# Triangular inversion in a recurrent layer: the second and third product of a level become one product of a buffer with itself

## The chip, the cores and the metric

The kernel runs on one core of a Trainium2 chip. The metric is the device time of one execution in microseconds (us); lower is better. The engines of the core are TensorE (PE; its weight loads are shown apart as PEld), VectorE (DVE), ScalarE (ACT), GpSimd (POOL) and the queues that issue transfers (SP's above all).

## The reference, cut to what matters

The whole program is three transformer blocks over 256 tokens of width 1024. The change lies in the first one, in the RWKV-7 recurrence of 8 heads with 64 columns each:

```
def step(state, inp):
    rt, wt, kt, vt, at, bt = inp
    sa = jnp.einsum('bhvk,bhk->bhv', state, at)
    state = state * wt[:, :, None, :] + sa[..., None] * bt[:, :, None, :] + vt[..., None] * kt[:, :, None, :]
    return state, jnp.einsum('bhvk,bhk->bhv', state, rt)
```

The kernel does not walk through the 256 tokens. It takes chunks of 128 tokens, builds for each of the 2 chunks x 8 heads a strictly triangular 128 x 128 matrix of the products between tokens, and needs the inverse of identity minus that matrix. These are 16 inverses.

## The kernel before

One program is written out for each engine; the engines meet at semaphores. The order on an engine is the order in which its functions are called, nothing is scheduled afterwards. The stage in question comes after the projections of the first block (`pe_mats` builds the 16 matrices) and before the recurrences (`pe_recurrences`), which use the inverses.

**The inversion** (`pe_inverse`, `act_inverse`, `dve_inverse`, `pool_inverse`) doubles the size of the inverted diagonal blocks in seven levels, 1, 2, 4 up to 64 on a side. The 16 matrices are handled as `NG` = 4 groups of four; a group is one instruction of 128 x 512 on DVE, ACT or POOL, and on TensorE four fp32 matmuls of 128 x 128, of which each shows as two passes in the profile (8 rows of LDWEIGHTS and MATMUL). `TI` holds the inverse so far, `TJ` its transpose, `AAB` the matrices. Per level from 1 on, for each group:

- POOL masks `AAB` with the block pattern of the level into `ALA` (L1087). It may write once the first product of the level before has been read.
- First product (L1098): `ALA` times `TI` into PSUM. It waits for the mask and for `TI` of the level before.
- ACT copies all of it to `PP` (L1125), once `TJ` of the level before is there too.
- Second product (L1109): `PP` with `TJ`. Third product (L1116): `TJ` with `PP`, its transpose. Level 6 has no third product, since `TI` isn't needed behind it.
- DVE adds the third to `TI` (L1157) and the second to `TJ` (L1159), each 128 x 512, from PSUM and SBUF.

On TensorE all four groups' first products stand ahead of the second and third ones of the level. At the head of levels 2 and 3 DVE also works off `dve_bonus` (L1133, L1137, L1139, L1141), four operations of 128 x 512 between SBUF buffers that prepare the layer's output and have nothing to do with the inversion; they stand in its queue before the additions of that level. The eight PSUM banks are taken in turn. `SM` is a small buffer of 64 columns of constants. `sp_start` issues the early loads on SP's queue, the constants (L722) among them, behind the vectors (L701 to L720) and ahead of the small weights of the layer.

Of the kernel before, what the change touches and what calls it, by code (L numbers as in the profile page):

```python
# [7 lines left out]
P = 128  # L8
# [5 lines left out]
ALU = mybir.AluOpType  # L14
# [12 lines left out]


NAMES = (["ident", "cinc", "cexc", "strict", "incl", "heads"]
         + [f"lvl{i}" for i in range(7)] + [f"acc{i}" for i in range(7)] + ["after", "upto", "ones", "swap"])  # L30
COLS = {n: 128 * i for i, n in enumerate(NAMES)}
WIDE = 128 * len(NAMES)

# [1 line left out]
def constants():  # L35
    s = np.arange(128)[:, None]
    t = np.arange(128)[None, :]
    out = {"ident": s == t, "strict": s < t, "incl": s <= t, "heads": s // 64 == t // 64,
           "cinc": (s <= t) * 1.0 - (s < 64), "cexc": (s < t) * 1.0 - (s < 64),
           "after": s > t, "upto": s <= t, "ones": (s >= 0) & (t >= 0), "swap": s == (t + 64) % 128}  # L40
    for i in range(7):
        m = 1 << i
        same = s // (2 * m) == t // (2 * m)
        right = (t // m) % 2 == 1

        out[f"lvl{i}"] = same & right & ((s // m) % 2 == 0)
        edge = t // (2 * m) * (2 * m) + m

        out[f"acc{i}"] = np.where(right, (s >= edge) & (s <= t), (s > t) & (s < edge))
    return np.concatenate([out[n].astype(np.float32) for n in NAMES], 1)  # L50
# [143 lines left out]
def program(nc, a):  # L194
    ctx = ExitStack()
    with ctx:
# [14 lines left out]
        XL = sb("XL", [P, 8, S], F32R)  # L211
        XT = (XH, XL)
        TF = sb("TF", [P, 2, 512])
        CST = sb("CST", [P, WIDE])
        VEC = sb("VEC", [P, 2, P])
        GB = sb("GB", [P, 2, D])
        SM = sb("SM", [P, 64])
# [453 lines left out]
        def group(x, g):  # L671
            return x[:, 4 * g:4 * g + 4, :]
# [20 lines left out]
        def sp_start(e):  # L693
# [13 lines left out]
            for r, name, n in ((0, "rwkv_mu", 1792), (15, "rwkv_k_k", 512), (19, "rwkv_k_a", 512),  # L707
# [11 lines left out]
                        ).then_inc(*up("rows", by=16))  # L719
            e.dma_start(VR[112:120, 1, :], a["c_2"].rearrange("a (r p) -> (a r) p", p=P)  # L720
                        ).then_inc(*up("rows", "rows", by=16))
            e.dma_start(CST[:, P:], a["consts"][:, P:]).then_inc(*up("consts", "consts", by=16))  # L722
            e.dma_start(GW2[0:16, :], a["gla_gate_w2"][0]).then_inc(*up("even", by=16))
            e.dma_start(W2A2[0:64, :], a["rwkv_w2"][0]).then_inc(*up("even", by=16))
            e.dma_start(W2A2[64:128, :], a["rwkv_a2"][0]).then_inc(*up("even", by=16))
# [346 lines left out]
                k.then_inc(*up("masked", use, ("free", use)))  # L1072


        def pool_inverse(e):
            for lv in range(7):
                for g in range(NG):
                    if lv == 0:
                        e.wait_ge(*at(("m", 4 * g + 3)))
                        if g == 0:  # L1080
                            e.wait_ge(*at(("bt", 3)))
                            e.wait_ge(*at(("la", 1)))
                    else:
                        e.wait_ge(*at(("p done", lv - 1, g)))
                        if lv == 1:
                            e.wait_ge(*at(("tj", 0, g)))
                    e.tensor_tensor(group(ALA, g), group(AAB, g), bc(f"lvl{lv}"), ALU.mult).then_inc(  # L1087
                        *up("level", ("al", lv, g)))

        def pe_inverse(e):  # L1090
            for lv in range(7):
# [9 lines left out]
                if lv == 0:  # L1101
                    continue
                for g in range(NG):
                    b = bank(e, ("j", lv, g))
                    e.wait_ge(*at(("pp", lv, g)))
                    if g == NG - 1:
                        e.wait_ge(*at(("tj", lv - 1, g)))
                    for s in range(4):
                        k = e.matmul(b[:, s * P:s * P + P], group(PP, g)[:, s, :], TJ[:, 4 * g + s, :],  # L1109
                                     start=True, stop=True)  # L1110
                    if lv == 6:
                        k.then_inc(*up("inverse", ("full", ("j", lv, g))))
                        continue
                    b = bank(e, ("i", lv, g))
                    for s in range(4):
                        k = e.matmul(b[:, s * P:s * P + P], TJ[:, 4 * g + s, :], group(PP, g)[:, s, :],  # L1116
                                     start=True, stop=True)
                    k.then_inc(*up("inverse", ("full", ("i", lv, g)), ("full", ("j", lv, g))))

        def act_inverse(e):  # L1120
            for lv in range(1, 7):
                for g in range(NG):
                    e.wait_ge(*at(("full", ("p", lv, g))))
                    e.wait_ge(*at(("tj", lv - 1, g)))
                    e.activation(group(PP, g), four(("p", lv, g)), ACT.Copy).then_inc(  # L1125
                        *up("levels", ("pp", lv, g), ("free", ("p", lv, g))))

        def dve_bonus(e, t):
# [14 lines left out]
        def dve_inverse(e):  # L1143
# [7 lines left out]
            for lv in range(1, 7):  # L1151
                if lv in (2, 3):
                    dve_bonus(e, lv - 2)
                for g in range(NG):
                    e.wait_ge(*at(("full", ("j", lv, g))))
                    if lv < 6:
                        e.tensor_tensor(flat(group(TI, g)), ps(("i", lv, g)), flat(group(TI, g)), ALU.add).then_inc(  # L1157
                            *up("tij", ("ti", lv, g), ("free", ("i", lv, g))))
                    e.tensor_tensor(flat(group(TJ, g)), ps(("j", lv, g)), flat(group(TJ, g)), ALU.add).then_inc(  # L1159
                        *up("tij", ("tj", lv, g), ("free", ("j", lv, g))))  # L1160


        def pe_chunk(e, step):
# [1350 lines left out]
```

## Time and profile before

| | us |
|---|---|
| time before, median of 3 runs (1250.09 to 1251.1) | 1250.32 |
| the profiled execution, its own time | 1247.66 |
| its span | 1245.7 |
| from the first second product to the end of the inversion on TensorE | 163.9 to 221.2 |
| TensorE busy over the whole span | 1128.2 (91%) |
| DVE, ACT, POOL busy | 742.0, 519.2, 120.8 |

The profile shows one execution. Shares of busy time are averages over the whole program; what bounds one stage is read from the rows of that stage: from the chain of work that ended last, the timelines of the engines, and the table by stretches. A granted clock of 1.00 means TensorE at 2.4 GHz, 0.50 means 1.2 GHz.

### The profile page before, as it was taken

What the parts mean: (1) busy time and instruction counts of PE and PEld (TensorE: products, weight loads), DVE (VectorE), ACT (ScalarE), POOL (GpSimd) and SP (SyncE); (2) the same over time, 40 slices, a digit from 0 to 9 for tenths busy, and PEclk for the clock granted to TensorE, in tenths of its full rate; (3) what the DMA queues carried; (4) which work ended last, traced back from release to release, by engine and by line L of the source; (5) the groups of instructions that cost most, each with busy time, mean ns of one, the idle gap of its engine ahead of it and who ended that gap; (6) DMA issues with size and microseconds to landing.
All of it is one profiled execution on the core that took longest, in us unless ns stands there. A gap on an engine that the chain in (4) does not pass through costs nothing.

```text
span 1245.7 us, 17256 instructions
## 1 busy us (share of the span) xinstructions
PE 1128.2 (91%) x7196; PEld 997.8 (80%) x7196; DVE 742.0 (60%) x1046; ACT 519.2 (42%) x710; POOL 120.8 (10%) x115
## 2 busy tenths in 40 slices
PE   5989799996799999977979499999969996999997
PEld 5788699995699998756767399998749875999885
DVE  3486585437676666566664666666574565666433
ACT  3452422124444443334564344343355565555331
POOL 0005163210300000040000300000010000000000
PEclk8899999958799999987999799999979997999999
DMA  8345000004398677531693287768615322565550
GB/s 279 101 123 184 16 2 1 1 1 163 107 300 273 210 262 273 203 120 53 182 195 123 83 285 243 242 235 299 230 40 182 105 88 68 171 195 177 203 169 34
DMA packets 112270, 193.68 MB, mean 155 GB/s; under 512 B 4514, under 2 KB 84913, under 8 KB 112066
## 3 DMA queue, kind: packets, MB, share of 16 engines
q1 hardware_dynamic: 108530, 179.65, 43.2%
q0 software_dynamic: 3248, 11.83, 4.3%
q8 instruction: 57, 0.93, 0.3%
q10 hardware_dynamic: 416, 1.11, 0.2%
q14 instruction: 19, 0.16, 0.0%
HBM read 188.38 MB, written 4.19 MB: 155 GB/s over the span
## 4 chain that ended last, share of the span: by engine, by line
PE 82%; DVE 10%; ACT 5%; issue 2%; SPq 1%; DMA 0%; POOL 0%; ACTq 0%; DVEq 0%
PE ps L406 22%; PE ps L407 21%; PE ps L408 21%; PE ps L1098 2%; PE ps L1868 2%; PE ps L1109 2%; PE ps L1853 2%; PE ps L1116 1%; DVE XL L539 1%; PE ps L1335 1%; DVE ARR L390 1%; DVE AR L1071 1%; PE ps L1846 1%; DVE STAT L556 1%; PE ps L1290 1%
## 5 line engine op out<-in xcount | busy, mean ns | idle before, releaser
L390 DVE TENSOR_TENSOR ARR<-ring,ARR 128x2048 fp32r<-128x2048 f32 (+1 forms) x147 | 329.3, 2246 | 220.9 <-ACT ARR L379 220.8
L406 PE MATMUL ps<-XH,ARR 128*128 128x256 f32 x1232 | 354.9, 288 | 25.6 <-DVE ARR L390 13.4
L379 ACT ACTIVATE ARR<-ring 128x2048 fp32r<-128x2048 f32 (+1 forms) x147 | 274.8, 1875 | 214.8 <-PE ps L408 163.5
L407 PE MATMUL ps<-XL,ARR 128*128 128x256 f32 x1232 | 351.9, 286 | 0.0
L408 PE MATMUL ps<-XH,ARR 128*128 128x256 f32 x1232 | 351.4, 285 | 0.0
L406 PEld LDWEIGHTS ps<-XH,ARR 128*128 128x128 f32 x1232 | 238.2, 193 | 30.9 <-issue 27.9
L407 PEld LDWEIGHTS ps<-XL,ARR 128*128 128x128 f32 x1232 | 238.4, 194 | 0.1
L408 PEld LDWEIGHTS ps<-XH,ARR 128*128 128x128 f32 x1232 | 238.2, 193 | 0.0
L406 PE MATMUL ps<-ARR 128*128 128x512 f32 x420 | 170.4, 406 | 9.1 <-DVE ARR L491 5.8
L407 PE MATMUL ps<-ARR 128*128 128x512 f32 x420 | 167.2, 398 | 0.0
L408 PE MATMUL ps<-ARR 128*128 128x512 f32 x420 | 167.1, 398 | 0.0
L406 PEld LDWEIGHTS ps<-ARR 128*128 128x128 f32 x420 | 80.0, 191 | 34.7 <-issue 9.5
L408 PEld LDWEIGHTS ps<-ARR 128*128 128x128 f32 x420 | 79.9, 190 | 19.0
L407 PEld LDWEIGHTS ps<-ARR 128*128 128x128 f32 x420 | 80.0, 190 | 18.2 <-issue 0.5
L406 PE MATMUL ps<-ARR,XH 128*128 128x512 f32 (+1 forms) x128 | 50.8, 397 | 7.0 <-DVE XL L539 5.4
L1513 DVE SCALAR_TENSOR_TENSOR AR<-ring,AR 128x1024 f32<-128x1024 f32 x42 | 53.9, 1283 | 1.1
L407 PE MATMUL ps<-ARR,XH 128*128 128x512 f32 (+1 forms) x128 | 49.9, 390 | 0.0
L408 PE MATMUL ps<-ARR,XL 128*128 128x512 f32 (+1 forms) x128 | 49.6, 388 | 0.0
L1603 ACT ACTIVATE ARR<-XN 128x512 fp32r<-128x512 f32 x22 | 13.9, 632 | 79.9 <-DVE XN L1621 79.9
L469 PE MATMUL ps<-CST,XN 128*128 128x128 f32 x96 | 18.6, 353 | 31.3 <-ACT XN L2071 19.4
L469 PEld LDWEIGHTS ps<-CST,XN 128*128 128x128 f32 x96 | 14.6, 182 | 35.5 <-ACT XN L2071 20.7
L1087 POOL TENSOR_TENSOR AR<-AR,CST 128x512 f32<-128x512 f32 x28 | 37.6, 1365 | 47.1 <-DVE AR L1071 25.3
(335 smaller groups left out, 1337.3 us busy)
## 6 DMA issues: line engine op xcount, KB each, us to landing
ring<-in_ffn_w_gate_up_dram SPq DMA_DIRECT2D x44, 1024.0 KB, 5.7
ring<-in_w_dram SPq DMA_DIRECT2D x32, 1024.0 KB, 5.2
ring<-in_w_ada_dram SPq DMA_DIRECT2D x24, 1024.0 KB, 5.3
ring<-in_ffn_w_down_dram SPq DMA_DIRECT2D x22, 1024.0 KB, 5.1
ring<-in_even_w_in_dram SPq DMA_DIRECT2D x13, 1024.0 KB, 5.6
ring<-in_w_in_dram SPq DMA_DIRECT2D x9, 1024.0 KB, 5.4
ring<-in_mla_w_q_b_dram SPq DMA_DIRECT2D x6, 768.0 KB, 4.7
ring<-in_even_w_out_dram SPq DMA_DIRECT2D x4, 1024.0 KB, 4.9
```

The costliest lines, as they stand in the source:

```text
L379: e.activation(split(i)[0], raw(i), ACT.Copy).then_inc(*up("hi", ("hi", i)))
L390: e.tensor_tensor(lo, raw(i), hi.bitcast(F32), ALU.subtract).then_inc(*up("lo", ("lo", i), ("raw free", i)))
L406: e.matmul(out, lhs[0], rhs[0], start=first, stop=False)
L407: e.matmul(out, lhs[0], rhs[1], start=False, stop=False)
L408: return e.matmul(out, lhs[1], rhs[0], start=False, stop=last)
L469: k = e.transpose(ps((tag, c // 2))[:, o:o + P], src[:, t, c * P:(c + 1) * P], ident)
L1087: e.tensor_tensor(group(ALA, g), group(AAB, g), bc(f"lvl{lv}"), ALU.mult).then_inc(*up("level", ("al", lv, g)))
L1098: k = e.matmul(b[:, s * P:s * P + P], ALA[:, 4 * g + s, :], ident if lv == 0 else TI[:, 4 * g + s, :], start=True, stop=True)
L1109: k = e.matmul(b[:, s * P:s * P + P], group(PP, g)[:, s, :], TJ[:, 4 * g + s, :], start=True, stop=True)
L1513: k = e.scalar_tensor_tensor(acc, w[:, c, :], CSL[:, k0 + c:k0 + c + 1], acc, ALU.mult, ALU.add)
L1853: k = e.matmul(b[:, TILE[t]], A.q_of(i, t), A.k_of(i, P * (t + 1)), start=True, stop=True)
L1868: k = e.matmul(ps((A.tag, "o", g))[64 * (h % 2):64 * (h % 2) + 64, o + P * t:o + P * t + P], A.v_of(h, j), px[:, (t + j) * P:(t + j) * P + ...
```

## The change

From level 1 on, `PP` becomes a buffer of two interleaved sides. At level `lv` the columns of a matrix are cut in blocks of `1 << lv`; the even blocks are side 0, the odd ones side 1. ACT writes side 1 of `PP` from side 1 of `TJ` (SBUF to SBUF) and side 0 from side 0 of the first product (PSUM to SBUF). TensorE multiplies this buffer with itself: one product per group in place of two. Its columns of side 1 carry what the second product gave and those of side 0 what the third gave, each in the rows of the other side; the remaining rows hold products that are not wanted. DVE adds the two halves with a mask by rows: a scalar_tensor_tensor that multiplies by a column of zeros and ones from `SM` and adds, 128 x 256 each. The masks are 14 new columns of the constants, which come with a transfer of their own on SP's queue.

```diff
+            e.dma_start(CST[:, P:], a["consts"][:, P:WIDE - P]).then_inc(*up("consts", by=16))
+            e.dma_start(SM[:, 8:22], a["consts"][:, COLS["sides"]:COLS["sides"] + 14]).then_inc(
+                *up("consts", "consts", by=16))
...
+        def side(x, lv, which):
+            return x.rearrange("p s (b w t) -> p s b w t", w=2, t=1 << lv)[:, :, :, which, :]
+
+        def rows_on(lv, which):
+            return SM[:, 8 + 2 * lv + which:9 + 2 * lv + which]
...
                 for g in range(NG):
-                    b = bank(e, ("j", lv, g))
+                    b = bank(e, ("ji", lv, g))
                     e.wait_ge(*at(("pp", lv, g)))
-                    if g == NG - 1:
-                        e.wait_ge(*at(("tj", lv - 1, g)))
                     for s in range(4):
-                        k = e.matmul(b[:, s * P:s * P + P], group(PP, g)[:, s, :], TJ[:, 4 * g + s, :],
-                                     start=True, stop=True)
-                    if lv == 6:
-                        k.then_inc(*up("inverse", ("full", ("j", lv, g))))
-                        continue
-                    b = bank(e, ("i", lv, g))
-                    for s in range(4):
-                        k = e.matmul(b[:, s * P:s * P + P], TJ[:, 4 * g + s, :], group(PP, g)[:, s, :],
-                                     start=True, stop=True)
-                    k.then_inc(*up("inverse", ("full", ("i", lv, g)), ("full", ("j", lv, g))))
+                        w = PP[:, 4 * g + s, :]
+                        k = e.matmul(b[:, s * P:s * P + P], w, w, start=True, stop=True)
+                    k.then_inc(*up("inverse", ("full", ("ji", lv, g))))
...
         def act_inverse(e):
             for lv in range(1, 7):
                 for g in range(NG):
+                    e.wait_ge(*at(("tj", lv - 1, g)))
+                    e.activation(side(group(PP, g), lv, 1), side(group(TJ, g), lv, 1), ACT.Copy).then_inc(*up("levels"))
+                for g in range(NG):
                     e.wait_ge(*at(("full", ("p", lv, g))))
-                    e.wait_ge(*at(("tj", lv - 1, g)))
-                    e.activation(group(PP, g), four(("p", lv, g)), ACT.Copy).then_inc(
+                    e.activation(side(group(PP, g), lv, 0), side(four(("p", lv, g)), lv, 0), ACT.Copy).then_inc(
                         *up("levels", ("pp", lv, g), ("free", ("p", lv, g))))
...
                 for g in range(NG):
-                    e.wait_ge(*at(("full", ("j", lv, g))))
+                    use = ("ji", lv, g)
+                    e.wait_ge(*at(("full", use)))
                     if lv < 6:
-                        e.tensor_tensor(flat(group(TI, g)), ps(("i", lv, g)), flat(group(TI, g)), ALU.add).then_inc(
-                            *up("tij", ("ti", lv, g), ("free", ("i", lv, g))))
-                    e.tensor_tensor(flat(group(TJ, g)), ps(("j", lv, g)), flat(group(TJ, g)), ALU.add).then_inc(
-                        *up("tij", ("tj", lv, g), ("free", ("j", lv, g))))
+                        x = side(group(TI, g), lv, 0)
+                        e.scalar_tensor_tensor(x, side(four(use), lv, 0), rows_on(lv, 1), x, ALU.mult, ALU.add).then_inc(
+                            *up("tij", ("ti", lv, g)))
+                    x = side(group(TJ, g), lv, 1)
+                    e.scalar_tensor_tensor(x, side(four(use), lv, 1), rows_on(lv, 0), x, ALU.mult, ALU.add).then_inc(
+                        *up("tij", ("tj", lv, g), ("free", use)))
```

TensorE at level 1 before, from the last two first products on (L1098), with the second (L1109) and third products (L1116) of the groups in turn:

```order
672 L1098 MATMUL ps<-AR 128x128 [waits s_tij,s_level,s_masked]
673 L1098 MATMUL ps<-AR 128x128 x3
674 L1109 MATMUL ps<-AR 128x128 [waits s_levels,s_tij]
675 L1109 MATMUL ps<-AR 128x128 x3
676 L1116 MATMUL ps<-AR 128x128 [waits s_tij]
677 L1116 MATMUL ps<-AR 128x128 x3
678 L1109 MATMUL ps<-AR 128x128 [waits s_levels,s_tij]
679 L1109 MATMUL ps<-AR 128x128 x3
```

TensorE at the same place now; L1110 is the first product and L1120 the product of `PP` with itself:

```order
672 L1110 MATMUL ps<-AR 128x128 [waits s_tij,s_level,s_masked]
673 L1110 MATMUL ps<-AR 128x128 x3
674 L1120 MATMUL ps<-AR 128x128 [waits s_levels,s_tij]
675 L1120 MATMUL ps<-AR 128x128 x3
676 L1120 MATMUL ps<-AR 128x128 [waits s_levels,s_tij]
677 L1120 MATMUL ps<-AR 128x128 x3
678 L1120 MATMUL ps<-AR 128x128 [waits s_levels,s_tij]
679 L1120 MATMUL ps<-AR 128x128 x3
680 L1120 MATMUL ps<-AR 128x128 [waits s_levels,s_tij]
681 L1120 MATMUL ps<-AR 128x128 x3
682 L1110 MATMUL ps<-AR 128x128 [waits s_tij,s_level,s_levels]
```

The first products of the next level follow after four products instead of eight.

ACT before, over all six levels: one copy per group and level (L1125).

```order
72 L1039 ACTIVATE XN<-XN,SM 128x256 [waits s_low]
73 L1125 ACTIVATE AR<-ps 128x512 [waits s_tij,s_inverse] x24
74 L1302 ACT_TABLE_LOAD [waits s_inverse]
```

ACT now at levels 1 to 3: L1127 copies the side of `TJ`, L1130 that of the first product.

```order
73 L1127 ACTIVATE AR<-AR 128x128x2 [waits s_tij] x4
74 L1130 ACTIVATE AR<-ps 128x128x2 [waits s_inverse] x4
75 L1127 ACTIVATE AR<-AR 128x64x4 [waits s_tij] x4
76 L1130 ACTIVATE AR<-ps 128x64x4 [waits s_inverse] x4
77 L1127 ACTIVATE AR<-AR 128x32x8 [waits s_tij] x4
```

All four copies of `TJ`, which wait for DVE's last addition of the level before, now stand ahead of the copies of the first products.

## Rows read from the trace of the kernel before

**Rows 1.** The page: busy time, share of the span, instructions of each engine.

```profile
PE 1128.2 (91%) x7196; PEld 997.8 (80%) x7196; DVE 742.0 (60%) x1046; ACT 519.2 (42%) x710; POOL 120.8 (10%) x115
```

**Rows 2.** The chain that ended last, levels 1 and 2: start, us, what.

```profile
164.07 0.89 PE ps L1109 x8
164.96 0.89 PE ps L1116 x8
...
171.21 3.57 PE ps L1098 x32
...
221.24 1.79 PE ps L1290 x16
```

**Rows 3.** Timeline of TensorE: start, us, engine, line, form, count.

```profile
163.90 1.06 PE L1109 MATMUL ps<-AR 128*128 128x128 f32 x8
...
171.05 1.17 PE L1098 MATMUL ps<-AR 128*128 128x128 f32 x9
```

**Rows 4.** Groups by line and shape from 163.9 to 221.2: busy us, mean ns.

```profile
L1116 PE MATMUL ps<-AR 128*128 128x128 f32 x160 | 21.1, 275 | 0.0
...
L1125 ACT ACTIVATE AR<-ps 128x512 f32<-128x512 f32 x21 | 12.5, 597 | 43.0 <-PE ps L1098 43.0
...
L1137 DVE TENSOR_TENSOR AR<-AR 128x512 f32<-128x512 f32 x2 | 3.3, 1644 | 0.1
```

**Rows 5.** Timeline of DVE around the extra work of levels 2 and 3.

```profile
171.25 0.69 DVE L1157 TENSOR_TENSOR AR<-ps,AR 128x512 f32<-128x512 f32 x1 [0.50 <-PE ps L1116]
171.86 0.68 DVE L1159 TENSOR_TENSOR AR<-ps,AR 128x512 f32<-128x512 f32 x1
172.46 1.55 DVE L1133 TENSOR_TENSOR AR<-AR 128x512 f32<-128x512 f32 x1
...
178.98 0.68 DVE L1157 TENSOR_TENSOR AR<-ps,AR 128x512 f32<-128x512 f32 x1
...
183.16 0.67 DVE L1159 TENSOR_TENSOR AR<-ps,AR 128x512 f32<-128x512 f32 x1
183.76 0.97 DVE L1133 TENSOR_TENSOR AR<-AR 128x512 f32<-128x512 f32 x1
...
189.70 0.68 DVE L1157 TENSOR_TENSOR AR<-ps,AR 128x512 f32<-128x512 f32 x1
```

**Rows 6.** Timeline of POOL, the masks of levels 3 to 5.

```profile
172.19 6.32 POOL L1087 TENSOR_TENSOR AR<-AR,CST 128x512 f32<-128x512 f32 x4 [4.45 <-PE ps L1098]
182.91 6.32 POOL L1087 TENSOR_TENSOR AR<-AR,CST 128x512 f32<-128x512 f32 x4 [4.40 <-PE ps L1098]
193.63 4.96 POOL L1087 TENSOR_TENSOR AR<-AR,CST 128x512 f32<-128x512 f32 x4 [4.40 <-PE ps L1098]
```

**Rows 7.** Groups elsewhere with the shapes and kinds that the change adds.

```profile
L795 DVE SCALAR_TENSOR_TENSOR AR<-AR,VEC 128x256 f32<-128x256 f32 x14 | 6.8, 485 | 0.5
...
L1258 DVE TENSOR_TENSOR XN<-XN,AR 128x512 f32<-128x512 f32 x2 | 1.4, 692 | 0.1
...
L1724 DVE TENSOR_TENSOR AR<-AR 128x256 f32<-128x256 f32 x2 | 0.8, 419 | 0.0
...
L1241 ACT ACTIVATE XN<-ps 128x256 f32<-128x256 f32 x4 | 1.5, 383 | 13.3 <-PE ps L1203 8.9 <-PE ps L1200 4.4
```

**Rows 8.** Busy us by stretch: PE, PEld, DVE, ACT, POOL; granted clock, DMA, GB/s.

```profile
152.00:155.40 3.40, 1.36 (x10) 1.20 (x11) 3.40 (x11) 0.00 (x0) 1.26 (x1) 1.00 0.00 0
155.40:158.80 3.40, 3.33 (x16) 3.06 (x15) 3.40 (x5) 0.00 (x0) 2.41 (x2) 0.50 0.00 0
158.80:162.20 3.40, 2.47 (x18) 1.95 (x17) 2.63 (x3) 1.25 (x3) 2.02 (x3) 1.00 0.00 0
...
244.10:281.70 37.60, 37.60 (x168) 33.78 (x170) 13.29 (x22) 6.71 (x9) 7.50 (x6) 0.50 0.00 1
```

**Rows 9.** SP's queue, and the chain's first users of the constants (L823).

```profile
13.73 0.36 SPq L722 DMA_DIRECT2D CST<-in_consts_dram  x1
...
41.57 1.05 PE ps L823 x2
```

More of the change, by code:

```diff
@@ L29 @@
 NAMES = (["ident", "cinc", "cexc", "strict", "incl", "heads"]
-         + [f"lvl{i}" for i in range(7)] + [f"acc{i}" for i in range(7)] + ["after", "upto", "ones", "swap"])
+         + [f"lvl{i}" for i in range(7)] + [f"acc{i}" for i in range(7)] + ["after", "upto", "ones", "swap", "sides"])
 COLS = {n: 128 * i for i, n in enumerate(NAMES)}
@@ L39, in constants @@
            "cinc": (s <= t) * 1.0 - (s < 64), "cexc": (s < t) * 1.0 - (s < 64),
-           "after": s > t, "upto": s <= t, "ones": (s >= 0) & (t >= 0), "swap": s == (t + 64) % 128}
+           "after": s > t, "upto": s <= t, "ones": (s >= 0) & (t >= 0), "swap": s == (t + 64) % 128,
+           "sides": (s >> np.minimum(t // 2, 6)) % 2 == t % 2}
     for i in range(7):
@@ L213, in program @@
         TF = sb("TF", [P, 2, 512])
-        CST = sb("CST", [P, WIDE])
+        CST = sb("CST", [P, WIDE - P])
         VEC = sb("VEC", [P, 2, P])
@@ L721, in sp_start @@
                         ).then_inc(*up("rows", "rows", by=16))
-            e.dma_start(CST[:, P:], a["consts"][:, P:]).then_inc(*up("consts", "consts", by=16))
+            e.dma_start(CST[:, P:], a["consts"][:, P:WIDE - P]).then_inc(*up("consts", by=16))
+            e.dma_start(SM[:, 8:22], a["consts"][:, COLS["sides"]:COLS["sides"] + 14]).then_inc(
+                *up("consts", "consts", by=16))
             e.dma_start(GW2[0:16, :], a["gla_gate_w2"][0]).then_inc(*up("even", by=16))
```

## The prediction

> **What bounds the kernel now.** I read the page first: TensorE is busy for 91% of the span [rows 1]. Then the chain of waits at the place of the change: from 163 us to 221 us it never leaves TensorE. Per level it shows four first products of 0.89 us (3.57 us in one piece), then second and third products in turn, 0.89 us each, eight of them, and straight behind the inversion the next stage's matmuls [rows 2]. So a level takes 12 x 0.893 = 10.72 us, and a product removed here is time removed, as long as the other engines keep up with the shorter level. The groups by line and the timelines say how busy they are: DVE's additions take 0.69 us each [rows 5], POOL's masks 1.2 to 1.6 us [rows 6], ACT's copies 0.597 us, and of these 57 us ACT idles 43 waiting for first products [rows 4]. The timelines of DVE and POOL also show the one place where they are nearly full: the extra work in levels 2 and 3 [rows 5, 6].
>
> **What is removed.** The third products, levels 1 to 5, four groups each: 20 groups (160 passes in the rows [rows 4]) x 0.893 us = 17.9 us, all of it on the path. The product that stays has the size of the second one, with the buffer on both sides; nothing in the rows gives a reason for another duration. The level becomes 8 x 0.893 = 7.15 us. Level 6 had no third product and keeps its length. Now the engines that must follow in 7.15 us.
>
> **DVE, ordinary levels.** Two scalar_tensor_tensor of 128 x 256 per group replace two additions of 128 x 512. The trace doesn't show this form with PSUM and short runs. Nearest: a scalar_tensor_tensor of 128 x 256 with a column operand, 0.485 us; an addition of 128 x 256 whose output steps over every second element (rotary embedding), 0.419 us [rows 7]; the old 512-wide one, 0.69 us [rows 5], as the upper end. I take 0.485. Additions in a row start 0.61 us apart at 0.69 us each (171.25, 171.86 [rows 5]), so 0.08 overlaps and the new ones start 0.40 apart. A group costs 0.80, below the 0.893 of its product; a level 3.2 us of 7.15. `TI` of group 3 is done 0.2 + 0.49 = 0.7 us after the last product's slot (0.2 as from 171.05 [rows 3] to 171.25 [rows 5]), but TensorE wants it only after three further first products, 2.7 us. Cost nothing; cover gone, it would be 0.7 us per level.
>
> **ACT.** Eight copies of 128 x 256 at 0.383 us [rows 7] are 3.1 us of 7.15; at the 0.597 of the old copy, 4.8. They stand in a new order: all four of `TJ` first, the last of which waits for DVE's last addition. That is done 0.2 + 0.40 + 0.49 = 1.1 us into the first products; then one `TJ` copy and one copy of a first product end at 1.9 us (2.3 at the upper end), and the product with itself starts at 3.57. Nothing again, hidden behind four first products. What waits behind it is the release of the first product's PSUM bank, wanted eight products later.
>
> **POOL.** Four masks take 5.0 us undisturbed and 6.3 us beside DVE's extra work [rows 6], below 7.15. They start about 1.1 us into the level (172.19 against 171.05) and are wanted one level on. Nothing.
>
> **DVE in levels 2 and 3** is where I expect part of the gain to stay. The four extra operations run from 172.46 to 178.98, 6.5 us, and the second time from 183.76 to 189.70, 5.9 us [rows 5], against a level that is now 7.15 us and also wants 3.2 us of additions. By hand, in times of this execution: the first product with itself can start at 163.9, where the second product started; four take 3.6 us, so level 2's first products start at 167.5 instead of 171.05 [rows 3]. DVE starts level 1's last additions at 167.7, the extra work at 168.5, and ends it at 175.0. The first `TI` is done at 175.5; level 3's first product could start at 174.65. **Stall 0.9 us.** Eight additions follow; the second extra work starts at 175.0 + 3.2 = 178.2. Level 4's first product could start at 175.55 + 7.15 = 182.7. If the extra work takes 5.9 us again, `TI` is done at 184.6, a stall of 1.9. But it is POOL that makes these operations slow (1.64 us [rows 4], a like one elsewhere 0.692 [rows 7]), and POOL now starts its masks at 176.7, 1.5 us ahead of the extra work instead of 0.85 us, and is done earlier with respect to it; I take 5.5 us. **Stall 1.5 us.** Bounds: 1.0 (5.0 us) and 2.5 (6.5 us, as the first time). Behind each stall the late `TJ` lets the product with itself begin with the fourth first product's end at best: 0 to 0.2 us more. From level 4 on the spare time above applies.
>
> At this place the rows say that additions from PSUM take 0.67 to 0.69 us whether POOL runs (183.16) or not (171.25), and that SBUF-only ones don't [rows 5, 6]. The Trainium skill, page "SBUF — State Buffer", section "Summary: rules for kernel authors", gives a harder rule: when a VectorE instruction has two SBUF inputs and GpSimd reads SBUF, the second to issue waits until the first has finished. An estimate by that rule would put full masks and extra operations end to end, some 6.0 us for the second extra work, a stall of 2.0 instead of 1.5 and a time 0.5 us above mine. The first time, end to end would be 4 x 1.24 + 4 x 0.61 = 7.4 us; the trace has 6.8 (172.19 to 178.98 [rows 5, 6]), so the rule is a little too hard here.
>
> **The early transfer.** 14 columns for 128 partitions on SP's queue cost one issue, 0.36 us in the row ahead of it [rows 9], ahead of the small weights and of the fourth ring load. Those weights are first used at 41.6 us [rows 9], more than 20 us later. Bounds 0 and 0.4 us; I take 0.1. `SM` is otherwise untouched, and banks are taken in turn as before, the last eight before the recurrences being again level 6's.
>
> **Sum.** 17.9 - 0.9 - 1.5 - 0.2 (the products behind the stalls, the transfer) = 15.3 us. Behind the inversion the chain stays on TensorE [rows 2], which is busy for all of the 37.6 us from 244.1 on [rows 8], and the next stage's loads are released by the same queues, so the gain should pass to the end undiminished. The profiled execution would go from 1247.66 to 1232.4; the runs' median, 2.7 us above it, from 1250.32 to **1235.0 us**. With my bounds (stalls 1.9 to 3.4 us, 0 to 0.4 behind them, transfer 0 to 0.4) 1234.3 to 1236.6; with the 512-wide duration for the additions, see the second rival, 1238.5.
>
> **Rivals.**
>
> 1. *The clock behind the inversion falls or returns at other work.* It falls at 244.1 and comes back at 281.7 us, 37.6 us at half speed with TensorE on the chain [rows 8]. The work arrives 15 us earlier, so the change of clock may meet other matmuls. Each us of full-clock work moved into or out of that stretch is worth 1 us. Against a large effect: what precedes the fall (small matmuls behind a wait for DVE) stays the same work, and the three runs lie within 1.0 us. For: the stretch is long, and there is denser work within it. An earlier return by 3 to 10 us of work gives 1225 to 1232 (chance 0.07); a later one or an earlier fall, 2 to 5 us, gives 1237 to 1240 (0.08).
>
> 2. *DVE becomes the pace.* If the new operation costs 0.69 us, starts lie 0.60 apart: 1.2 us per group against 0.893. The first `TI` comes 0.2 later, the second extra work starts 1.6 later, and the fourth `TI` holds the fourth first product by about 0.9 in both levels: together near 3.6 us, 1238.5. If it also had to take turns with POOL, as the SBUF-only operations do at 1.64 instead of 0.69 [rows 4, 7], four masks would add up to 4 x 0.95 = 3.8 us to DVE's 3.2 in an ordinary level, 7.0 of 7.15, and some 2 us to each of levels 2 and 3: 1239. Against: its first input is PSUM, as in the additions that POOL doesn't slow. Chance 0.07.
>
> 3. *Slower than before: the stalls cost the clock.* After a stretch in which TensorE worked only 1.36 of 3.4 us the clock fell for 3.4 us; after one with 2.47 of 3.4 the products ran on at full speed [rows 2, 8]. My stalls (0.9 and 1.5 us in long dense work) resemble the second. If the fall came at level 4 and stayed, as it does from 244 on, the 24 products left (21.4 us) would take 21.4 us more: 1235.0 + 21.4 = 1256. The point from which the change loses is 15.3 us of full-clock work done at half. Against: dense products brought the clock back at once at 158.8. Chance 0.03; a single short fall, worth 1.7 us, lies in my range.
>
> 4. *It doesn't do what it says:* a wait elsewhere takes the gain, the inversion being shorter but the recurrences starting when they did. Nothing in the chain behind 221.2 comes from another engine's earlier work [rows 2]. 1248 to 1252, chance 0.02.
>
> **How the numbers follow.** The forecast, 1233 to 1237, has 0.73; the rivals 0.15, 0.07, 0.03, 0.02. The range 1230 to 1239 takes in the first, most of the second and the near half of the clock cases, and leaves out some 0.15. Time can be told from no change here beyond 0.2%, 2.5 us. Faster: 0.73 + 0.15 + 0.07 = 0.95; within 0.2%: 0.02; slower: 0.03.
>
> **What would show it.** The chain between 160 and 206 us all TensorE but for two short pieces with DVE, before the first products of levels 3 and 4; the product with itself at 0.89 us per group, 192 passes; scalar_tensor_tensor near 0.485 us at every level, the one with runs of two elements included; the inversion ending near 206 us; the stretch at half clock again about 37 us. Wrong would be: an addition above 0.6 us, a stall of TensorE in levels 5 or 6, or a span behind the inversion that is not the old one.

## The result and the profile after

| | before | changed |
|---|---|---|
| median of 4 runs, us | 1250.2 (1250.08 to 1251.1) | 1232.74 (1232.04 to 1233.0) |
| the profiled execution, its own time | 1247.66 | 1232.66 |
| its span | 1245.7 | 1230.8 |

The ratio is 0.9858 with a 95% interval of 0.9841 to 0.9875: 17.5 us faster, where 15.3 were forecast. The profiled executions differ by 15.0 us. That these two numbers are not the same turned out to be the interesting part.

The timeline of TensorE after the change (start, us, engine, line, form, count), from the last passes of level 1's first products to the next stage (L1298), answers to [rows 3]; L1110 is the first product, L1120 the product of `PP` with itself:

```profile
162.87 3.74 PE L1120 MATMUL ps<-AR 128*128 128x128 f32 x32
166.44 3.74 PE L1110 MATMUL ps<-AR 128*128 128x128 f32 x32
170.02 3.74 PE L1120 MATMUL ps<-AR 128*128 128x128 f32 x32
173.69 3.81 PE L1110 MATMUL ps<-AR 128*128 128x128 f32 x32
177.34 3.74 PE L1120 MATMUL ps<-AR 128*128 128x128 f32 x32
182.58 3.81 PE L1110 MATMUL ps<-AR 128*128 128x128 f32 x32 [1.51 <-DVE AR L1164]
186.23 3.74 PE L1120 MATMUL ps<-AR 128*128 128x128 f32 x32
...
204.10 1.95 PE L1298 MATMUL ps<-CST,AR 128*128 128x128 f32 x16
```

Starts of the blocks lie 3.57 us apart: a level takes 7.15 us, as worked out. Two places are longer. Level 3's first products start at 173.69 where 170.02 + 3.57 = 173.59 was possible, and level 4's at 182.58 instead of 177.34 + 3.57 = 180.91: stalls of 0.10 and 1.67 us, with 0.08 us behind each where the product with itself follows (177.34 - 173.69 = 3.65). The inversion from its first such product to the next stage takes 204.1 - 162.9 = 41.2 us. Before it was 221.1 - 163.9 = 57.2 us [rows 2, 3]. The stage gave 16.0 us.

DVE's timeline (same columns) shows the two pieces of extra work (L1138 to L1146) between the masked additions (L1164, L1167), to be read against [rows 5]:

```profile
167.05 0.47 DVE L1167 SCALAR_TENSOR_TENSOR AR<-ps,SM,AR 128x256 f32<-128x256 f32 x1
167.44 0.68 DVE L1138 TENSOR_TENSOR AR<-AR 128x512 f32<-128x512 f32 x1
168.15 1.64 DVE L1142 TENSOR_TENSOR AR<-AR 128x512 f32<-128x512 f32 x1
...
173.07 0.47 DVE L1164 SCALAR_TENSOR_TENSOR AR<-ps,SM,AR 128x256 f32<-128x256 f32 x1
...
176.21 1.75 DVE L1138 TENSOR_TENSOR AR<-AR 128x512 f32<-128x512 f32 x1
...
181.35 0.69 DVE L1146 TENSOR_TENSOR AR<-AR 128x512 f32<-128x512 f32 x1
181.96 0.48 DVE L1164 SCALAR_TENSOR_TENSOR AR<-ps,SM,AR 128x256 f32<-128x256 f32 x1
```

POOL's masks at the same places, the counterpart of [rows 6]:

```profile
167.58 6.69 POOL L1099 TENSOR_TENSOR AR<-AR,CST 128x512 f32<-128x512 f32 x4 [0.86 <-PE ps L1110]
174.90 5.86 POOL L1099 TENSOR_TENSOR AR<-AR,CST 128x512 f32<-128x512 f32 x4 [0.63 <-PE ps L1110]
```

The first extra work takes 173.07 - 167.44 = 5.6 us instead of the 6.5 of before, since its first operation now starts 0.14 us ahead of POOL's mask and runs in 0.68 us; before, POOL started 0.27 us ahead (172.19, 172.46 [rows 5, 6]) and it took 1.55. The second takes 181.96 - 176.21 = 5.75 us. Which of its four operations is the fast one can change from run to run: here the last took 0.69 us and the first 1.75, in the third trace of this kernel the first took 0.68 and the last 1.64, though POOL had started 1.31 us ahead in both.

Groups by line and shape inside the inversion (count, then busy us, mean ns, idle us before them and its releaser), the counterpart of [rows 4]:

```profile
L1120 PE MATMUL ps<-AR 128*128 128x128 f32 x192 | 22.4, 275 | 0.0
...
L1110 PE MATMUL ps<-AR 128*128 128x128 f32 x162 | 19.2, 276 | 1.5 <-DVE AR L1164 1.5
...
L1167 DVE SCALAR_TENSOR_TENSOR AR<-ps,SM,AR 128x256 f32<-128x256 f32 x23 | 10.9, 475 | 4.4 <-PE ps L1120 4.4
L1164 DVE SCALAR_TENSOR_TENSOR AR<-ps,SM,AR 128x256 f32<-128x256 f32 x20 | 9.6, 479 | 9.5 <-PE ps L1120 9.3
L1127 ACT ACTIVATE AR<-AR 128x256 f32<-128x256 f32 x20 | 8.3, 417 | 19.0 <-DVE AR L1167 19.0
L1130 ACT ACTIVATE AR<-ps 128x256 f32<-128x256 f32 x21 | 7.5, 379 | 5.0 <-PE ps L1110 5.0
```

The passes that are left kept their 275 ns, the additions take 0.48 us, the copies 0.38 and 0.42 us.

The rest of the span moved too. It is best read in three parts, each bounded by a start on TensorE:

| profiled execution, us | before | changed | difference |
|---|---|---|---|
| up to the first second product / product with itself | 163.9 | 162.9 | -1.0 |
| the inversion from there | 57.2 | 41.2 | -16.0 |
| from the next stage's start to the end | 1024.6 | 1026.7 | +2.1 |

Nothing in the first and third part was changed but one small transfer. Their granted clock differs. By stretches (start and end, length, then PE, PEld, DVE, ACT, POOL busy; granted clock, DMA share, GB/s), first early in the program, before:

```profile
15.00:22.30 7.30, 6.04 (x29) 6.04 (x30) 2.69 (x6) 0.00 (x0) 0.00 (x0) 0.53 0.94 308
```

The same stretch after:

```profile
15.00:22.30 7.30, 6.22 (x35) 6.23 (x36) 2.51 (x6) 0.00 (x0) 0.00 (x0) 1.00 0.98 293
```

And behind the inversion, before (its long half-clock stretch is in [rows 8]) and then after:

```profile
281.70:298.70 17.00, 8.60 (x65) 7.41 (x63) 15.97 (x24) 9.33 (x24) 1.18 (x2) 0.80 0.45 154
```

```profile
204.10:225.60 21.50, 20.70 (x181) 19.57 (x179) 11.98 (x18) 3.75 (x7) 8.94 (x5) 1.00 0.00 1
225.60:263.10 37.50, 37.50 (x155) 33.19 (x155) 11.63 (x19) 6.69 (x9) 4.80 (x3) 0.50 0.00 0
263.10:283.60 20.50, 11.95 (x86) 10.77 (x84) 18.24 (x27) 9.46 (x25) 3.87 (x5) 0.75 0.36 131
```

Early on, the execution of before ran 29 passes, nearly all at half clock, where the changed one ran 35 at full clock. That this makes the 1.0 us of the first part is not shown: over the 14 traces of this document that part takes 162.8 to 164.2 us without following its time at half clock (23.9 to 30.7 us; the shortest start has 30.7).

Behind the inversion the half-clock stretch is as long (37.5 against 37.6 us) and begins 21.5 instead of 23.0 us behind its end; a further piece at half clock follows. Summed from the trace's clock record to the end, the third part holds 148.5 us at half clock in place of 144.8. In the run with all extra work in one level (below) 3.4 us at half clock cost dense matmuls 1.7 us; an estimate at that rate gives 1.8 of the 2.1 us.

### The profile page after: what moved, and what is told of

Read it like the earlier page. It is cut to its first block, busy times and chain, and to the rows that moved or that the text cites. A ratio compares the mean times of both kernels' runs of the same rounds, so it can differ in the third digit from the quotient of the medians.

```text
span 1230.8 us, 16937 instructions
## 1 busy us (share of the span) xinstructions
PE 1110.9 (90%) x7036; PEld 981.1 (80%) x7036; DVE 732.1 (59%) x1046; ACT 522.8 (42%) x734; POOL 120.7 (10%) x115
## 4 chain that ended last, share of the span: by engine, by line
PE 80%; DVE 11%; ACT 5%; issue 2%; SPq 1%; DMA 0%; POOL 0%; ACTq 0%; DVEq 0%
PE ps L407 22%; PE ps L408 21%; PE ps L409 21%; PE ps L1876 2%; PE ps L1861 2%; PE ps L1110 1%; DVE XL L540 1%; PE ps L1343 1%; DVE ARR L391 1%; DVE AR L1074 1%; PE ps L1854 1%; PE ps L1120 1%; DVE STAT L557 1%; PE ps L1298 1%; ACT ARR L380 1%
## 5 line engine op out<-in xcount | busy, mean ns | idle before, releaser
L409 PEld LDWEIGHTS ps<-ARR 128*128 128x128 f32 x420 | 80.0, 190 | 18.8
L470 PE MATMUL ps<-CST,XN 128*128 128x128 f32 x96 | 18.3, 354 | 30.1 <-ACT XN L2079 12.6
L600 POOL TENSOR_TENSOR X<-XN,GB 128x1024 f32<-128x1024 f32 x6 | 14.1, 2343 | 279.4 <-ACT XN L578 279.4
```

The costliest lines, as they stand in the source:

```text
L409: return e.matmul(out, lhs[1], rhs[0], start=False, stop=last)
L470: k = e.transpose(ps((tag, c // 2))[:, o:o + P], src[:, t, c * P:(c + 1) * P], ident)
L600: e.tensor_tensor(X[:, t, :], XN[:, t, :], GB[:, 0, :], ALU.mult).then_inc(*up("affine"))
```

## The experiments

Two theories. **A**: the gain is the stage's, 17.9 us of products less the stalls behind DVE's extra work, and everything else only scatters. **C**: on top of it the change puts the end of the inversion at another offset to the changes of TensorE's clock, and with that the rest of the program gets systematically shorter or longer. In the expectations a rival B stands for the first form of C. "Stage" is the inversion as above and "rest" what follows it, both from the profiled execution; means are over all runs of a kernel.

### The changed kernel again

The same file, twice more, each time beside other runs of before.

> The changed kernel as it is, to see what of its gain belongs to the change and what to the clock's position in one execution. Theory A (17.9 us of products removed, 1.9 us given back in two stalls behind DVE's extra work, nothing elsewhere on average): 15.9 to 16 us faster than before, ratio 0.9872. Rival B (the gain is larger than the inversion's own, since behind it or ahead of it less is spent at half clock): the ratio stays at 0.986 or below, and the stretches at half clock are shorter in sum than before.

> The changed kernel once more, since its runs of the second job lay in two groups, spans of 1220 to 1225 and of 1233 us, while the stage takes 41.2 us in both traces. Theory A (stage alone): 16 us below before on average, 1232 to 1234. Theory C (on top of the stage, the work behind the inversion now more often meets the clock at a better offset, rest of the program 1019 us long instead of 1024 to 1028): mean 18 to 21 us below before, again in two groups.

Ratios 0.9833 (0.9798 to 0.9869) and 0.9851 (0.9822 to 0.988): the second mean lies 18.8 us below the runs of before beside it, as theory C had it and more than A's 16. The stage was 41.2 and 41.1 us, the rest 1027.6 and 1026.2 us in the profiled executions. Rival B's second sign, less time at half clock, is missing in these traces; both come from the slower group of runs. The runs lay at 1222.4 to 1226.7 (four) and 1234.7, 1234.9; then 1224.7, 1224.8 and 1232.1 to 1234.2 (four). The kernel before was not as steady either as its first runs had it: 63 more runs gave 1241.8 to 1252.5. Over all runs: changed 1230.0 (16 runs), before 1248.8 (67 runs), 18.7 us apart, of which the stage explains 16.0. The six runs of the changed kernel at 1222.4 to 1226.7 had a mean granted clock of 0.932 to 0.938, the other ten 0.927 to 0.934; none of the six was profiled.

### Only the products back

```diff
                         k = e.matmul(b[:, s * P:s * P + P], w, w, start=True, stop=True)
+                    if lv < 6:
+                        for s in range(4):
+                            w = PP[:, 4 * g + s, :]
+                            k = e.matmul(b[:, s * P:s * P + P], w, w, start=True, stop=True)
```

> The changed kernel with the product of the buffer with itself computed twice in levels 1 to 5, so TensorE has as much to do as before while ACT, DVE and the early transfer are those of the change. Theory A: 20 products of 0.893 us come back and cover the stalls: the time of before, 1250 us, within 1 us; the inversion 57.3 us. Rival (part of the gain comes from the smaller copies and additions, or from the clock): 2 us or more below the time of before.

Ratio 1.0009 (0.9992 to 1.0026), stage 57.2 us, exactly that of before. Its timeline of TensorE has the two products in turn and no stall, as in [rows 3]:

```profile
163.10 1.06 PE L1120 MATMUL ps<-AR 128*128 128x128 f32 x8
163.99 1.06 PE L1124 MATMUL ps<-AR 128*128 128x128 f32 x8
...
170.25 3.74 PE L1110 MATMUL ps<-AR 128*128 128x128 f32 x32
173.82 1.06 PE L1120 MATMUL ps<-AR 128*128 128x128 f32 x8
```

All of the stage's gain is in the 20 products; the smaller copies and additions bring nothing by themselves.

### Only the narrower additions

```diff
-                        e.tensor_tensor(flat(group(TI, g)), ps(("i", lv, g)), flat(group(TI, g)), ALU.add)
+                        x = side(group(TI, g), lv, 0)
+                        e.tensor_tensor(x, side(four(("i", lv, g)), lv, 0), x, ALU.add)
...
-                    e.tensor_tensor(flat(group(TJ, g)), ps(("j", lv, g)), flat(group(TJ, g)), ALU.add)
+                    x = side(group(TJ, g), lv, 1)
+                    e.tensor_tensor(x, side(four(("j", lv, g)), lv, 1), x, ALU.add)
```

> The kernel before with only its additions narrowed to the side that a level changes (128 x 256 instead of 128 x 512); three products, copies and transfers as before. Theory A: DVE is not on the chain of the stage, no change: within 1 us of 1250. Rival (the additions' width matters): 1 to 3 us faster.

Ratio 0.9997 (0.998 to 1.0015), stage 57.2 us. Its additions by group (columns as above):

```profile
L1164 DVE TENSOR_TENSOR AR<-ps,AR 128x256 f32<-128x256 f32 x23 | 9.6, 416 | 4.6 <-PE ps L1112 4.6
L1161 DVE TENSOR_TENSOR AR<-ps,AR 128x256 f32<-128x256 f32 x20 | 8.5, 424 | 27.2 <-PE ps L1119 27.1
```

DVE worked 0.42 us instead of 0.69 per addition and idled the difference (27.2 us before one of the two groups, 16.5 in the trace of before). It was not on the chain.

### Only the transfer

```diff
+            e.dma_start(SM[:, 8:22], a["consts"][:, COLS["sides"]:COLS["sides"] + 14]).then_inc(
+                *up("consts", "consts", by=16))
```

> The kernel before with only the new transfer of 14 mask columns on the SP queue and the shorter constants buffer. Forecast: 0 to 0.4 us slower, not to be told from no change. Rival: the transfer delays what follows on the queue or shifts the start, 1 us or more either way; the trace then shows the first second product at another time than 163.9 us.

Ratio 0.9994 (0.998 to 1.0009); the first second product starts at 163.3 us. The start in all the traces, with the transfer or without, lies between 162.8 and 164.2. So it costs nothing that can be seen, and a shift of 1 us either way, as the rival had it, is scatter that kernels without the transfer show too.

### DVE's extra work: spread, before and after the change

```diff
-                if lv in (2, 3):
-                    dve_bonus(e, lv - 2)
+                if lv in (2, 3, 4, 5):
+                    dve_bonus(e, (lv - 2) // 2, (0, 1) if lv % 2 == 0 else (2, 3))
```

where the last argument picks two of the four operations.

> The changed kernel with DVE's extra work (eight operations, four each at the head of levels 2 and 3) spread as two each over levels 2 to 5. Theory A: DVE then needs 3.3 + 3.2 us of a level's 7.15, both stalls (0.1 and 1.7 us) go, the inversion takes 39.5 us from the first product with itself to the next stage instead of 41.4, time 1.8 us below the changed kernel. Rival: the stall is not the extra work's but the new order on ACT (all copies of TJ ahead): then a stall of 1 to 2 us stays in levels 3 or 4 and the time is that of the changed kernel.

> The changed kernel with DVE's extra work as two operations each at the head of levels 2 to 5, again beside the changed kernel on one chip. Theory A: 1.9 us below the changed kernel in the mean, the stage 39.3 us again. Theory C: the stage is 1.9 us shorter for certain, but the mean of the whole lies within 3 us of the changed kernel either way, since the end of the inversion meets the clock at another offset.

> The kernel before with the extra work spread over levels 2 to 5. Theory A: it hid behind 10.7 us levels and costs nothing there, so the time stays 1250.2 within 1 us. Rival: it cost time before too, 1 us or more faster.

In the changed kernel both stalls go: every block of TensorE now lies 3.57 us behind the last, and the stage is 39.3 us in both traces, 1.9 less, as theory A had it:

```profile
170.49 3.74 PE L1120 MATMUL ps<-AR 128*128 128x128 f32 x32
174.06 3.74 PE L1110 MATMUL ps<-AR 128*128 128x128 f32 x32
177.63 3.74 PE L1120 MATMUL ps<-AR 128*128 128x128 f32 x32
181.21 3.74 PE L1110 MATMUL ps<-AR 128*128 128x128 f32 x32
```

That rules out the new order on ACT as the cause of the stall; it is unchanged here. The time of the whole is less clear. Ratios to before 0.9851 (0.9827 to 0.9875) and 0.9835 (0.9806 to 0.9865), mean 1228.8 over 12 runs against 1230.0 of the changed kernel: in the right direction, within the scatter. In the kernel before the same edit leaves the stage at 57.2 us and the time at 0.9997 (0.9982 to 1.0012): the extra work cost nothing while a level was 10.7 us long.

### All extra work in one level

```diff
-                if lv in (2, 3):
-                    dve_bonus(e, lv - 2)
+                if lv == 3:
+                    dve_bonus(e, 0)
+                    dve_bonus(e, 1)
```

> The changed kernel with all eight extra operations of DVE in front of level 3's additions instead of four each at levels 2 and 3. Theory A: DVE's 11 to 12 us of extra work start 1 us into level 3 and hold level 4's first product by some 5 to 6 us, in place of 0.1 and 1.7: 3.5 to 4.5 us above the changed kernel, if the clock stays. Rival (the prediction's third: a wait of this length makes the clock fall): a stretch at 0.50 behind the wait and 1.7 us or more on top, 1238 or above.

Mean 1236.0, 6.0 above the changed kernel, ratio 0.9902 (0.9878 to 0.9926); the trace is of the fastest of the six runs. The stage is 45.0 us, 3.7 above the changed kernel. The timeline of TensorE splits it:

```profile
178.15 3.74 PE L1120 MATMUL ps<-AR 128*128 128x128 f32 x32
185.69 5.44 PE L1110 MATMUL ps<-AR 128*128 128x128 f32 x32 [3.80 <-DVE AR L1165]
190.96 3.74 PE L1120 MATMUL ps<-AR 128*128 128x128 f32 x32
```

The first product starts at 185.69 instead of 181.72: 4.0 us of wait, not 5 to 6, since the last three extra operations ran at 0.69 us once POOL was done. Then the block needs 5.27 us to the next one's start instead of 3.57. So the 3.7 us are within what theory A expected, but made of 2.0 us of wait and 1.7 of something else. The table by stretches says of what (columns as above):

```profile
182.70:186.10 3.40, 0.41 (x4) 0.44 (x5) 3.30 (x7) 0.13 (x1) 0.00 (x0) 1.00 0.00 0
186.10:189.50 3.40, 3.40 (x19) 3.40 (x18) 2.18 (x6) 2.19 (x6) 1.65 (x2) 0.51 0.00 0
189.50:193.00 3.50, 3.50 (x33) 3.50 (x33) 0.93 (x3) 0.80 (x3) 3.33 (x3) 0.99 0.00 0
```

After 3.4 us in which TensorE worked 0.41, the clock was at half for 3.4 us, and back. A wait of 4 us cost 1.7 more in clock, while the changed kernel's stall of 1.67 cost none; where between the two the cost begins is not shown. This is the first link of the prediction's third rival; the second, that the clock stays down, did not happen between dense products. The whole stayed below the 1238 that the rival had for this case.

### Wider masked additions

```diff
-                        x = side(group(TI, g), lv, 0)
-                        e.scalar_tensor_tensor(x, side(four(use), lv, 0), rows_on(lv, 1), x, ALU.mult, ALU.add)
+                        x = flat(group(TI, g))
+                        e.scalar_tensor_tensor(x, ps(use), rows_on(lv, 1), x, ALU.mult, ALU.add)
```

and the same for `TJ`.

> The changed kernel with both masked additions over all 512 columns instead of the side's 256: this also adds the products' unwanted columns, so the inverses are not those of the reference; it prices the width. Theory A with the prediction's second rival: 0.69 us each and 0.61 apart, 1.2 us per group against 0.893: the second extra work starts 1.6 us later, and the fourth addition holds the fourth first product in levels 3 and 4; together 3.6 us above the changed kernel, 1236.3. Rival (covered by the first products as before): within 1 us of the changed kernel.

This kernel adds the unwanted columns of the products too, so its inverses are not the right ones and it serves as a price only. The stage is 46.0 us, 4.8 above the changed kernel; I had 3.6. An addition takes 0.74 us, not 0.69, and they start 0.66 apart, so in levels 3 and 4 the first products come at DVE's pace, one group per 1.32 us:

```profile
175.78 1.13 PE L1110 MATMUL ps<-AR 128*128 128x128 f32 x8 [1.53 <-DVE AR L1164]
177.10 1.13 PE L1110 MATMUL ps<-AR 128*128 128x128 f32 x8 [0.19 <-DVE AR L1164]
178.42 1.13 PE L1110 MATMUL ps<-AR 128*128 128x128 f32 x8 [0.19 <-DVE AR L1164]
```

So the halving of the additions, worth nothing alone, is worth 4.8 us once the product is gone. Yet the whole is 1230.0 in the median and 1232.7 in the mean, only 2.7 above the changed kernel. The stage and the whole part ways again, which leads to the last pair.

### The end of the inversion moved on purpose

Both kernels get matmuls computed twice at level 6, results unchanged; they only push the inversion's end. Before, five of them:

```diff
-                    for s in range(4):
+                    for s in [0, 1, 2, 3] + [0, 1, 2, 3, 0] * (lv == 6 and g == 0):
                         k = e.matmul(b[:, s * P:s * P + P], group(PP, g)[:, s, :], TJ[:, 4 * g + s, :],
```

> The kernel before with five matmuls of level 6 computed twice (1.12 us more of TensorE at the end of the inversion, result unchanged). It makes the inversion as long as to put its end at the same offset to the clock's changes as the changed kernel has. Theory A: 1.1 us slower than before, 1249.5 to 1250. Theory C: part of the runs has the short rest of 1019 us, so the mean falls below before by 1 to 4 us although work was added; a group of runs at 1240 to 1242.

The changed kernel, ten of them:

```diff
-                    for s in range(4):
+                    for s in [0, 1, 2, 3] + [0, 1, 2, 3] * (lv == 6 and g < 2) + [0, 1] * (lv == 6 and g == 2):
                         w = PP[:, 4 * g + s, :]
                         k = e.matmul(b[:, s * P:s * P + P], w, w, start=True, stop=True)
```

> The changed kernel with ten matmuls of level 6 computed twice (2.23 us more at the end of the inversion, result unchanged), which puts the inversion's end back at the offset to the clock's changes that it had before the change. Theory A: 2.2 us above the changed kernel in each of its groups, two groups as before. Theory C: the fast group thins out or goes, mean 4 to 7 us above the changed kernel, 13 to 14 us below before, runs between 1230 and 1237.

**The kernel before with 1.1 us more work is faster**: median 1242.9 against 1250.0, ratio 0.9966 (0.9944 to 0.9988), nine of its 12 runs between 1241.2 and 1243.5. Its stage is 58.3 us, as it must be; the rest is 1019.3 us instead of 1024.6. By stretches from the inversion's end on:

```profile
221.50:243.10 21.60, 20.80 (x181) 19.67 (x180) 12.14 (x18) 3.75 (x7) 8.94 (x5) 1.00 0.00 1
243.10:253.30 10.20, 10.20 (x40) 8.68 (x42) 1.54 (x3) 0.60 (x1) 0.86 (x1) 0.50 0.01 2
253.30:263.60 10.30, 10.30 (x82) 9.26 (x80) 7.44 (x13) 2.45 (x4) 2.71 (x2) 1.00 0.00 0
263.60:273.80 10.20, 10.20 (x52) 9.27 (x53) 3.85 (x6) 3.55 (x4) 2.90 (x3) 0.50 0.01 2
```

The clock falls 21.6 us behind the end as it did in the changed kernel's trace, but comes back after 10.2 us, where [rows 8] has 37.6 us at half clock without a break. Over the 90 us behind the inversion, first of the kernel before, then with the five:

```profile
221.10:311.10 90.00, 79.46 (x467) 70.93 (x466) 48.09 (x68) 23.47 (x44) 17.69 (x12) 0.75 0.17 55
```

```profile
221.50:311.50 90.00, 79.42 (x494) 69.83 (x493) 50.46 (x69) 24.50 (x44) 17.59 (x12) 0.83 0.19 64
```

The changed kernel with 2.2 us more went the other way: mean 1235.4, no run below 1232.8, which is 5.4 us for 2.2 us of work, ratio 0.9893 (0.9872 to 0.9913), rest 1028.3 us. Theory A had 1249.5 to 1250 for the first kernel and the lower group of runs still there in the second. The first result contradicts it clear of noise. The second is weaker by itself: six runs, and ten of the changed kernel's 16 lay above 1232 as well.

That it is the clock which makes the rest longer or shorter can be read from all 14 traces. The rest ranges from 1018.7 to 1028.3 us and its time at half clock from 131.6 to 152.1 us. The rest less half of that time is 951.5 to 953.0 us in 13 of them and 954.5 in the other, whatever the kernel.

All kernels together. "At half clock" is how much of the rest the clock record has at half clock, "mean - stage" what the rest and the beginning take on average:

| kernel | runs | stage | rest in its trace | at half clock | mean | mean - stage |
|---|---|---|---|---|---|---|
| before | 67 | 57.2 | 1024.6 | 144.8 | 1248.8 | 1191.6 |
| products back | 12 | 57.2 | 1024.5 | 145.0 | 1249.2 | 1192.0 |
| narrower additions | 12 | 57.2 | 1026.5 | 148.2 | 1248.4 | 1191.2 |
| transfer alone | 12 | 57.2 | 1024.4 | 144.8 | 1248.0 | 1190.8 |
| before, spread | 10 | 57.2 | 1025.9 | 147.7 | 1248.0 | 1190.8 |
| before, five more | 12 | 58.3 | 1019.3 | 134.1 | 1244.7 | 1186.4 |
| changed | 16 | 41.2 | 1026.7, 1027.6, 1026.2 | 148.5, 152.1, 148.8 | 1230.0 | 1188.8 |
| changed, ten more | 6 | 43.4 | 1028.3 | 152.1 | 1235.4 | 1192.0 |
| changed, spread | 12 | 39.3 | 1018.9, 1025.4 | 131.7, 141.8 | 1228.8 | 1189.5 |
| changed, wide additions | 6 | 46.0 | 1018.7 | 131.6 | 1232.7 | 1186.7 |
| changed, one level | 6 | 45.0 | 1019.9 | 134.6 | 1236.0 | 1191.0 |

The five kernels with a stage of 57.2 us agree within 1.2 us in the last column, whatever they do in it. Those with another length range over 5.6 us. The change's 18.7 us are thus 16.0 of the stage and some 2.7 from outside it. The 2.7 are the difference of means over runs that spread by 12.6 us, so they are uncertain by about 2, and that they are the clock's is argued from the runs' granted clock, since no trace has the lower group.

That more or less work in front changes how much of the rest runs at half clock is shown by the kernel with five more matmuls. How is not settled; theory C's offset of the inversion's end to the clock's changes does not order the traces by itself. The first fall behind the inversion comes 21.5 to 24.8 us behind its end. In two traces it came at almost the same distance (21.5 and 21.6 us) and the clock stayed down for 37.5 us in one and 10.2 in the other; the four short rests have it at 21.6, 21.7, 23.6 and 23.6 us, and long ones have it at 21.5 and 23.4.

The version with the extra work spread has the shortest stage of all and is the one to keep; against the changed kernel its advantage is shown for the stage (1.9 us) and not for the whole.

## Why the prediction was right, point by point

The measured 1232.74 lies 2.3 us below the forecast and within its range. The stage was foreseen within 0.7 us by the right mechanism. That the whole lay in the range was in part luck: the mean of all 16 runs is 1230.0, its lower edge, and six of them lay below it; the first four all came from the slower group. The second set's median alone, 1225.9, would have been outside.

- **What is removed**: 17.9 us. Held to the last digit: 192 passes left, a level at 7.15 us.
- **DVE in ordinary levels, ACT, POOL**: 0.48 us per masked addition at every level, runs of two elements included (forecast 0.485); no wait of TensorE for ACT. The wider experiment shows that the cover was real and thin.
- **First stall**: forecast 0.9, measured 0.10. The failing term is the 6.5 us of the extra work, taken from a row in which POOL's mask started first. Shorter additions let DVE start it 1.0 us into the level instead of 1.4, ahead of POOL's 1.14, so one of four operations ran in 0.68 us: 5.6 us. The prediction asked this question for the second piece only, although its own times (DVE at 168.5, POOL 1.1 us behind 167.5) had the two change places.
- **Second stall**: forecast 1.5, measured 1.67, from 5.75 us of extra work (forecast 5.5). The Trainium skill's rule ("SBUF — State Buffer", "Summary: rules for kernel authors": the second to issue waits for the first to finish) gave an estimate of 6.0; the measurement lies midway. For the first piece, where DVE's operation issued first and took 0.68 us, the trace agrees with the rule that only the second one waits; my row had POOL first.
- **Behind the stalls and the transfer**: 0.2 forecast, 0.16 and nothing visible.
- **Sum of the stage**: 15.3 forecast, 16.0 measured.
- **"The gain should pass to the end undiminished"**: the weakest step. In the profiled pair 1.0 us came on top ahead of the stage and 2.1 were lost behind it; over all runs 2.7 came on top. The prediction had named a span behind the inversion that is not the old one as a sign of being wrong, and it came: 1026.7 against 1024.6. Rival 1 named the mechanism, and its 0.15 was too little: six of 16 runs lay where its earlier return (0.07) would put them, or lower, and the scatter stands beside the forecast, not in place of it. The argument against it that failed was "the three runs lie within 1.0 us": further runs of the same kernel spread over 10.7 us.
- **From the profiled execution to the median**: I added the 2.7 us by which the profiled execution of before lay below its median. The changed one's lay 0.1 below. That alone moves the result 2.6 us below the forecast, the stage 0.7 us more, and the profiled pair's remainder (-1.0 and +2.1) takes 1.1 back: together the 2.3 us between 1235.0 and 1232.74, within 0.1.
- **Rival 2** would have cost 4.8, not 3.6 us; **rival 3** was seen behind a wait of 4 us and not behind one of 1.67, and lost 1.7 us there and not 21; **rival 4** did not occur.

## What to carry to other kernels

When a product leaves a chain, the engines that idled beside it become the next question; work out for each what it must do in the shorter period, and look for one-off work in its queue. For two engines that slow each other, a duration from the trace may not hold once their order changes: the same operation took 1.55 us behind POOL's start and 0.68 ahead of it. Judge a change of 1 to 2% by the length of its stage in two traces as well as by the whole, since what follows moved here by up to 9.6 us on the clock alone.

## What the runs showed of the hardware that I had not expected

- The same work behind the inversion took between 1018.7 and 1028.3 us, by how much of it (131.6 to 152.1 us) ran at half clock. Delaying it by 1.1 us of matmuls made the whole shorter, by 7 us in the median and 4 in the mean of the runs.
- The clock's changes are not tied to the start of the program: the kernel before had a half-clock stretch from 15.4 to 22.3 us, the changed one none until 44.7, with the same work there. The Trainium skill says so ("TensorE: Matmul & The Clock Gate", "Part 1: The HAM clock gate"): what watches the activity runs free of the kernel's start, and the same kernel starts cold for a varying number of matmuls. It also puts the penalty of such a start at less than 1% of a typical kernel and advises against fitting a count of cold matmuls. The falls behind the inversion are not a start; their spread here is 9.6 us, 0.8%, and yet more than half of the effect under study.
- A masked addition with a column operand takes 0.48 us at 256 columns and 0.74 at 512, against 0.42 and 0.69 of the plain one.
